# Splitting each weight unit in two halves, at its begin and at its middle, up to three units ahead of use

## What is computed

```python
def first_block(x, ...):
    for l in range(DEPTH):
        h = rms_norm(x, attn_norm[l])
        proj = h @ w_in[l]
        ...
        mixed = jnp.concatenate([out_a, out_b, out_c], axis=-1)
        x = x + mixed @ w_out[l]
        h = rms_norm(x, ffn_norm[l])
        x = x + (jax.nn.silu(h @ w_gate[l]) * (h @ w_up[l])) @ w_down[l]

def hybrid_layer(x, ...):
    h = rmsnorm(x, norm_mix)
    proj = h @ w_in
    ...
    y_a = from_heads(o_a) @ w_o_fox
    y_b = from_heads(o_n.reshape(B, NSA_HEADS, T, HEAD_DIM)) @ w_o_nsa
    mixed = jax.nn.sigmoid(gate_a) * y_a + jax.nn.sigmoid(gate_b) * y_b
    x = x + mixed @ w_out
    h = rmsnorm(x, norm_mlp)
    return x + jnp.square(jax.nn.relu(h @ w_up)) @ w_down
```

## Time and profile before

| | |
|---|---|
| median of three runs | 2856.04 us |
| time of the profiled execution | 2851.48 us |
| its span, first to last instruction | 2849.7 us |
| TensorE (PE) busy | 2730.9 us, 96% |
| VectorE (DVE) busy | 1556.9 us, 55% |
| ScalarE (ACT) busy | 1157.8 us, 41% |
| GpSimd (POOL) busy | 132.1 us, 5% |
| mean granted TensorE clock | 0.989 |
| transfers of w_up, w_down, w_gate (512 KB each) | 108, 108, 44 |

### The profile page before, as it was taken

The page is one execution under the profiler, slowest core; times in us unless marked ns, Lnnn a source line. Parts: engine busy times, 40 slices in busy tenths (PEclk is TensorE's granted clock), DMA queues, the critical chain, the costliest instruction groups (busy, mean ns, idle before and its releaser), DMA issues.

```text
span 2849.7 us, 34790 instructions
## 1 busy us (share of the span) xinstructions
PE 2730.9 (96%) x13497; PEld 2249.6 (79%) x13497; DVE 1556.9 (55%) x2788; ACT 1157.8 (41%) x2078; POOL 132.1 (5%) x221
## 2 busy tenths in 40 slices
PE   7899999999999999989899999999989899999997
PEld 6778888887788888767778888888768778888886
DVE  7856444467564444576766653343667665643343
ACT  3554222235542222355654433242465644342331
POOL 1000000000000000011122000000010211000000
PEclk9999999998999999999999999999999999999999
DMA  4102232321022323321311233333212211323332
GB/s 121 52 23 86 96 97 98 99 87 56 22 87 96 96 96 97 92 67 54 103 45 45 90 95 96 97 98 99 88 45 89 68 45 60 104 90 98 99 99 75
DMA packets 186358, 231.40 MB, mean 81 GB/s; under 512 B 11874, under 2 KB 140356, under 8 KB 186196
## 3 DMA queue, kind: packets, MB, share of 16 engines
q1 hardware_dynamic: 184500, 225.95, 25.4%
q0 software_dynamic: 976, 1.32, 0.3%
q10 hardware_dynamic: 720, 1.92, 0.2%
HBM read 227.05 MB, written 2.11 MB: 80 GB/s over the span
## 4 chain that ended last, share of the span: by engine, by line
PE 79%; DVE 12%; ACT 5%; issue 3%; DMA 0%; POOL 0%; ACTq 0%; DVEq 0%
PE bank L641 23%; PE bank L643 23%; PE bank L642 23%; DVE Wl L2192 2%; ACT Wh L1466 1%; PE bank L901 1%; PE bank L846 1%; DVE STT L2500 1%; PE bank L922 1%; PE bank L923 1%; PE bank L964 1%; PE bank L831 1%; PE bank L1155 1%; PE bank L965 1%; DVE KAl L2240 1%
## 5 line engine op out<-in xcount | busy, mean ns | idle before, releaser
L2192 DVE TENSOR_TENSOR Wl<-RAW,Wh 128x1024 fp32r<-128x1024 f32 (+3 forms) x434 | 510.5, 1199 | 367.1 <-ACT Wh L1466 366.2
L1466 ACT ACTIVATE Wh<-RAW 128x1024 fp32r<-128x1024 f32 (+3 forms) x434 | 437.7, 1032 | 402.7 <-PE bank L643 402.2
L641 PE MATMUL bank<-Hh,Wh 128*128 128x512 f32 (+1 forms) x1104 | 450.4, 408 | 6.3 <-DVE Wl L2192 4.9
L643 PE MATMUL bank<-Hh,Wl 128*128 128x512 f32 (+1 forms) x1104 | 433.3, 393 | 0.0
L642 PE MATMUL bank<-Hl,Wh 128*128 128x512 f32 (+1 forms) x1104 | 433.1, 392 | 0.0
L641 PE MATMUL bank<-HA,Wh 128*128 128x512 f32 x704 | 274.2, 390 | 0.0
L642 PE MATMUL bank<-HA,Wh 128*128 128x512 f32 x704 | 273.9, 389 | 0.0
L643 PE MATMUL bank<-HA,Wl 128*128 128x512 f32 x704 | 273.9, 389 | 0.0
L641 PEld LDWEIGHTS bank<-Hh,Wh 128*128 128x128 f32 (+1 forms) x1104 | 208.1, 188 | 48.9 <-DVE Wl L2192 6.2
L643 PEld LDWEIGHTS bank<-Hh,Wl 128*128 128x128 f32 (+1 forms) x1104 | 207.2, 188 | 46.9
L642 PEld LDWEIGHTS bank<-Hl,Wh 128*128 128x128 f32 (+1 forms) x1104 | 208.2, 189 | 36.3
(11 more groups left out here) (394 smaller groups left out, 4690.2 us busy)
## 6 DMA issues: line engine op xcount, KB each, us to landing
RAW<-in_w_up_dram SPq DMA_DIRECT2D x108, 512.0 KB, 3.6
RAW<-in_w_down_dram SPq DMA_DIRECT2D x108, 512.0 KB, 3.7
RAW<-in_w_in_dram SPq DMA_DIRECT2D x90, 512.0 KB, 3.5
RAW<-in_w_gate_dram SPq DMA_DIRECT2D x44, 512.0 KB, 3.6
RAW<-in_w_out_dram SPq DMA_DIRECT2D x28, 512.0 KB, 3.7
RAW<-in_cmp_w_dram SPq DMA_DIRECT2D x16, 512.0 KB, 3.8
RAW<-in_w_o_fox_dram SPq DMA_DIRECT2D x8, 512.0 KB, 3.4
RAW<-in_w_o_nsa_dram SPq DMA_DIRECT2D x8, 512.0 KB, 3.4
```

Source lines behind the costliest of these rows:

```text
L641: pe.matmul(o, sh, mh, start=first, stop=False)
L643: return pe.matmul(o, sl, mh, start=False, stop=last)
L1466: sc.activation(M.Wh[:, v % NHL, 0:n], M.RAW[:, v % NRAW, 0:n], ACT.Copy).then_inc(G.w_hi, 1)
L2192: ve.tensor_tensor(M.Wl[:, v % NRAW, 0:n], M.RAW[:, v % NRAW, 0:n], M.Wh[:, v % NHL, 0:n].bitcast(F32), ALU.subtract).then_inc(G.w_lo, 1)
```

## The change

Two things change on ScalarE and VectorE, and one constant on TensorE's wait. A unit is split by two instructions, one for each half of its columns (split_halves), with the first half at the begin of a unit and the second at its middle: before j = 1 in lin_t, before s = 2 in lin_s. The semaphores w_hi and w_lo now count halves, and TensorE waits for both. AHEAD is 3: the first half of unit u+3 is due at the begin of unit u, its second half at the middle of u. Where a unit has no middle, its half is done at the next begin, ahead of the first half that is due there. The waits for the raw weights and for a free Wh buffer stand before the first half. The numbers of buffers, the loads and TensorE's order of work stay.

```diff
--- before.py
+++ after.py
@@ -34,7 +34,7 @@
 U = 1024
 NRAW = 5
 NHL = 4
-AHEAD = 2
+AHEAD = 3
 
 
 C_ID, C_J, C_CM, C_IF, C_ED, C_IW, C_NC, C_NS, C_CC, C_CS, C_XM, C_XV, C_SE, C_END = np.cumsum(
@@ -633,7 +633,7 @@
         u = unit[0]
         unit[0] += 1
         kt, pitch = unit_of(plan, u)
-        pe.wait_ge(G.w_lo, u + 1)
+        pe.wait_ge(G.w_lo, 2 * u + 2)
         h, lo = (w[:, 0:kt * pitch].rearrange("p (t n) -> p t n", n=pitch) for w in (M.Wh[:, u % NHL, :], M.Wl[:, u % NRAW, :]))
         return u, h, lo, kt
 
@@ -1452,25 +1452,36 @@
     hi, sq, ex = Count(G.part_hi), Count(G.sq), Count(G.ex)
     mx, a_mul, a_sq = Count(G.mx), Count(G.a_mul), Count(G.a_sq)
 
+    def split_halves(m):
+
+        while cut[0] < min(m, 2 * len(plan)):
+            v, h = divmod(cut[0], 2)
+            cut[0] += 1
+            kt, pitch = unit_of(plan, v)
+            n = kt * pitch // 2
+            c = slice(h * n, h * n + n)
+            if h == 0:
+                sc.wait_ge(G.raw_in[v % NRAW], landed(plan, v))
+                if v >= NHL:
+                    sc.wait_ge(*K.points["unit", v - NHL])
+            sc.activation(M.Wh[:, v % NHL, c], M.RAW[:, v % NRAW, c], ACT.Copy).then_inc(G.w_hi, 1)
+
     def next_unit():
         u = unit[0]
         unit[0] += 1
-        while cut[0] <= min(u + AHEAD, len(plan) - 1):
-            v = cut[0]
-            cut[0] += 1
-            kt, pitch = unit_of(plan, v)
-            n = kt * pitch
-            sc.wait_ge(G.raw_in[v % NRAW], landed(plan, v))
-            if v >= NHL:
-                sc.wait_ge(*K.points["unit", v - NHL])
-            sc.activation(M.Wh[:, v % NHL, 0:n], M.RAW[:, v % NRAW, 0:n], ACT.Copy).then_inc(G.w_hi, 1)
+        split_halves(2 * (u + AHEAD) + 1)
         return unit_of(plan, u)[0]
+
+    def second_half():
+        split_halves(2 * (unit[0] + AHEAD))
 
     def lin_t_units(name, kt, evac, before=None):
         k0 = 0
         while k0 < kt:
             ku = next_unit()
             for j in range(2):
+                if j:
+                    second_half()
                 for k in range(ku):
                     if before:
                         before(k0 + k)
@@ -1491,6 +1502,8 @@
         while k0 < kt:
             ku = shared or next_unit()
             for s in range(NT):
+                if s == 2:
+                    second_half()
                 for k in range(ku):
                     if before:
                         before(k0 + k)
@@ -2180,24 +2193,34 @@
     sink_ex, mx, rec, whole = Count(G.sink_ex), Count(G.mx), Count(G.rec), Count(G.whole)
     cs, sn = M.CSI[:, 0, :, :], M.CSI[:, 1, :, :]
 
+    def split_halves(m):
+
+        while cut[0] < min(m, 2 * len(plan)):
+            v, h = divmod(cut[0], 2)
+            cut[0] += 1
+            kt, pitch = unit_of(plan, v)
+            n = kt * pitch // 2
+            c = slice(h * n, h * n + n)
+            ve.wait_ge(G.w_hi, cut[0])
+            ve.tensor_tensor(M.Wl[:, v % NRAW, c], M.RAW[:, v % NRAW, c], M.Wh[:, v % NHL, c].bitcast(F32),
+                             ALU.subtract).then_inc(G.w_lo, 1)
+
     def next_unit():
         u = unit[0]
         unit[0] += 1
-        while cut[0] <= min(u + AHEAD, len(plan) - 1):
-            v = cut[0]
-            cut[0] += 1
-            kt, pitch = unit_of(plan, v)
-            n = kt * pitch
-            ve.wait_ge(G.w_hi, v + 1)
-            ve.tensor_tensor(M.Wl[:, v % NRAW, 0:n], M.RAW[:, v % NRAW, 0:n], M.Wh[:, v % NHL, 0:n].bitcast(F32),
-                             ALU.subtract).then_inc(G.w_lo, 1)
+        split_halves(2 * (u + AHEAD) + 1)
         return unit_of(plan, u)[0]
+
+    def second_half():
+        split_halves(2 * (unit[0] + AHEAD))
 
     def lin_t_units(name, kt, evac, before=None):
         k0 = 0
         while k0 < kt:
             ku = next_unit()
             for j in range(2):
+                if j:
+                    second_half()
                 for k in range(ku):
                     if before:
                         before(k0 + k)
```

## The result

The changed kernel took 2858.18 us (median of 20 runs, 2856.19 to 2862.17), the kernel before 2854.97 us in 20 runs beside it (2851.41 to 2858.05). The ratio is 1.0014, interval 1.0008 to 1.0021: no gain but a small loss of some 3 us, clear of the noise, where 9 us of gain were forecast.

What follows compares the result with a forecast made beforehand. TensorE was taken as the bound, with gains possible only in attention stretches. Second block -6.8 and first block -2.2 gave -9.0 us, so 2847 us for the median 2856.0; range 2832 to 2863 us.

Steps and rivals of the forecast that it cites:

- The boundaries in nsa: Second block's token-to-block attention: half units shorten three TensorE stalls ahead of the compression's hidden units; 3.0 us per layer with a later stall.
- The compressed scores: Two compressed-score chains in nsa: the new middle piece delays TensorE up to 1.7 us, less boundary gains; 1.3 us lost per layer.
- Three ahead: Forget gates, second block: splitting three units ahead removes the 2.48 us stall but makes QA later; 1.0 us lost per layer.
- The first block's window attention: Four stalling boundaries gain 2.8 us, middles cost 1.25: about 1.6 us gained per layer.
- New waits and DMA: Later-freed Wh buffers and raw weight loads: no cost in attention because ScalarE trails; in feed-forward weights land 1.8 us early.
- The price of a piece: Each added split piece costs VectorE 0.05 to 0.15 us, taken as 0.1 on a full engine, hidden in feed-forward.
- The middles: New VectorE wait for ScalarE's second half at each ordinary unit's middle: costs nothing with slack, up to 1.31 us without.
- slower rival: ScalarE and VectorE tied together at every middle, 1.31 us each without slack; 14 more such middles give 2865 us; chance 0.12.
- The forecast of less idle time: TensorE's idle time in the middle of the run falls from about 90 to near 81 us.

Runs made afterwards that it cites:

- e2: The kernel before with AHEAD = 3 alone, whole units split at the begin: 2864.31 us, ratio 1.0036 to the kernel before.
- e3: The changed kernel without a middle in the stages that end in a norm (second half at the next begin): 2847.46 us, ratio 0.9976 to the kernel before.
- e5: The changed kernel with both halves split at the begin of the unit and AHEAD = 2: 2844.69 us, ratio 0.9964 to the kernel before.
- e4: The changed kernel with both halves split at the begin of the unit everywhere, three units ahead: 2848.28 us, ratio 0.9983 to the kernel before.
- e1: The changed kernel with AHEAD = 2, halves still at begin and middle: 2876.86 us, ratio 1.0077 to the kernel before.
- e6: Both halves at the begin, three ahead, with the middle put back only in the stages that end in a norm: 2859.21 us, ratio 1.0018 to the kernel before.
- e7: The changed kernel with the norm stages' second half at s = 1 instead of s = 2: 2861.02 us, ratio 1.0020 to the kernel before.

## Why the prediction was wrong

Each step against the rows of after:

- *The boundaries in nsa* were right at the first two. The stalls of 1.95, 1.99 and 1.63 us were forecast at about 1.4, 1.0 and 0.7 and are 1.42, 1.02 and 1.14; the third gave back 0.49 where I had 0.96:

```profile
1416.81 0.30 PE L901 MATMUL bank<-CST,P 128*128 128x128 f32 x1 [1.42 <-POOL P L3316]
...
1433.57 0.30 PE L901 MATMUL bank<-CST,P 128*128 128x128 f32 x1 [1.02 <-POOL P L3316]
...
1449.97 0.30 PE L901 MATMUL bank<-CST,P 128*128 128x128 f32 x1 [1.14 <-POOL P L3316]
```

- *The compressed scores* got longer as said, 10.0 us in four waits instead of 7.5, or 1.25 per layer. I had 1.3, though its terms, twice 1.7 less 0.8 to 0.97, give 1.5 to 1.8.
- *Three ahead.* The stall of 2.48 at 1229.94 went and QA came later, as described: 1.18 on the Wl of the next unit and 2.88 on QA, 4.06 together where 4.4 was forecast. I had not foreseen the slow stretch behind it (1252 to 1264, 2.7 us more in the ledger):

```profile
1248.09 0.50 PE L641 MATMUL bank<-Hh,Wh 128*128 128x512 f32 x1 [1.18 <-DVE Wl L2205]
...
1255.35 0.69 PE L964 MATMUL bank<-KAh,QA 128*128 128x384 f32 x1 [2.88 <-DVE QA L2265]
```

- *The first block's window attention* gained 1.6 us in the first layer, as forecast: the changed kernel is 2.2 us behind at 180 us and 0.6 at 228.
- *New waits and DMA* in feed-forward cost nothing: 50.00 us of 50 are busy there. But "in attention it costs nothing, because ScalarE trails" was read from one row, and e2 contradicts it: in out0 ScalarE's split is held 6.19 us for TensorE, and three ahead with whole units costs 9 us. A stall of 0.75 us of this kind is left in e3, and was in no term of my sum.
- *The price of a piece.* I had 575 us for VectorE's sum and 520 for ScalarE's; they are 565.8 and 507.2. In e5, where the halves stand back to back, the added piece costs (539.3 - 510.5) / 434 = 66 ns on VectorE and (477.9 - 437.7) / 434 = 93 ns on ScalarE. The Trainium skill ("Perfetto Trace Analysis", Optimizing Scalar/DVE Operations) gives about 60 and 93 ns, and this trace agrees.
- **The failed step is "The middles".** I bounded a middle by nothing and 1.31 us, placed the losses by the stalls that the trace of before already showed, and gave the other middles nothing. The out0 stage had no stall, so it did not enter. There both engines take turns on one chain, and the chain's end had no slack: 12.4 us lost in two layers. It is the mechanism of my slower rival ("ScalarE and VectorE are tied together at every middle"), but I had it decide by the number of stalling middles, from seven on. What decided was where they stood: the middles of one short stage per layer outweighed all that the others gained.
- **A second one was left out altogether.** I counted stalls only, as if TensorE's busy time were fixed. Behind the longer stalls its clock fell to 1.2 GHz for some microseconds, which about doubled the price (6.1 us more of stalls and 6.3 more of slow matmuls in the two out0 stretches).

The forecast of less idle time held (9 against 12.4), so did most of its terms. With the norm stages' middles left out, the kernel is at 2847.46, where I had put the changed one at 2847. That is partly chance: in that kernel the other middles gain little over both halves at the begin (e3 against e4, 0.8 us): e3 is better in nsa (5.3 against 7.7 us in the ledger) and in out0 (3.3 against 7.1, where it has no middle and 1.8 of e4's are slow matmuls of an earlier place), and worse in fox (3.3 against 1.0) and at the compressed scores (4.3 against 1.8). The gain that I credited to moving the halves is mostly that of cutting them.

Shown by experiment: that the middles of the norm stages cost 11 to 12 us, that halves at the same place gain only if VectorE may begin behind the first of them, and that without middles the third unit costs rather than gains. Only argued: how much of the loss is the clock. No run held the stalls and changed the clock alone. The runs of the kernel before bear on it: over the 42 distinct pairs of span and mean granted clock that they left, the span grows with the time lost to the clock, correlation 0.80, but by only 0.3 us for each microsecond lost. So slow matmuls don't always cost their length, and the 18.8 us of them are no price by themselves.

## What to carry to other kernels

When two engines hand a job to each other in program order, cut the job in pieces so that the second begins behind the first piece; that gave 9.4 us here without moving anything. Before a piece is moved into the middle of a stage, look there for a chain that ends just as its reader is free: it has no row among the waits, and its slack is to be read from the timeline. And compare busy times as well as idle times, since the same matmuls can take longer.

## What the runs showed of the hardware

- After a stall of 2.11 us the granted clock was 0.50 in a stretch of 4 us: 10 matmul records in it instead of 21. All eight stalls of 2.11 or 2.12 us of this chain, two each in after, e1, e6 and e7, have such a fall beside or behind them. The stalls of 0.75 in e3 and of 1.32 to 1.34 in e4 have none (e4's extra slow matmuls in layer 0 stand at 203 to 206 us, ahead of the stall). Of e2's two stalls of 1.33 one has it, in layer 1, and one has not. The first line is of e4 in layer 0, the second of e2 in layer 1; I could not tell a rule between 1.3 and 2.1 us.

```profile
260.00:264.00 4.00, 4.00 (x19) 3.31 (x18) 2.62 (x14) 0.00 (x0) 0.00 (x0) 1.00 0.12 18
```

```profile
834.00:838.00 4.00, 4.00 (x12) 3.09 (x11) 1.88 (x12) 0.00 (x0) 0.00 (x0) 0.57 0.02 4
```

- One kernel's runs spread by up to 9 us (2848.86 to 2857.63 in 20 runs of the kernel before), and their mean granted clock with them, from 0.990 in the fastest to 0.984 in the slowest. The profiled execution of the kernel before, at 0.989, was one of the faster ones.
- Matmuls at 1.2 GHz cost nothing where TensorE would have waited anyway: from 96 to 150 us, 4 us more of slow matmuls took the place of 4.7 us of stalls.
